# Moving 96 partition-swap DMAs of the attention stage from the GpSimd queue to the ScalarE queue

## The chip, the cores and the metric

The kernel runs on one core of a Trainium2 chip. The metric is the device time of one launch in microseconds. The engines are TensorE (PE), VectorE (DVE), ScalarE (ACT), GpSimd (POOL) and SyncE (SP). Each has its own program, and they meet only at semaphores.

## The reference, cut to what matters

The whole program is two transformer blocks over 512 tokens of width 1024: a convolution layer, a dilated-attention layer, gates and feed-forward layers. The change touches one step of the dilated attention, the partial rotation of the queries and keys:

```
q, k, v, gate = split(h @ w_in)                 # three groups of 8 heads of 64
q = partial_rope(rms_norm(q, q_norm), cos, sin) # k alike
def partial_rope(x, cos, sin):                  # only the first 16 of 64 rows turn
    x1, x2 = x[..., :8], x[..., 8:16]
    rot = concat([x1 * c - x2 * s, x2 * c + x1 * s])
    return concat([rot, x[..., 16:]])
```

The kernel keeps features on partitions and tokens along the free axis, so one 128x512 array holds two heads of 64 rows. To add `x2 * s` to `x1 * c`, rows 8 to 15 of each head have to come to the partitions of rows 0 to 7, and the other way round. DVE and ACT work within a partition, so a DMA makes that swapped copy.

## The kernel before, in words

Weights stream from HBM in 299 tiles of 512 KB through a ring of four buffers. For each tile SP issues the load, ACT writes the rounded half `w_hi` (its `prep`), DVE writes the rest `w_lo` (its `prep`), and PE multiplies three products per 128-column part. ACT and DVE work three tiles ahead of PE.

The attention stage (`begin(k, 4)` in each engine's program, about 340 to 700 us) is written as steps `c` from 0 to 4 with ten slots `j` each. In steps 0 to 3, PE projects one tile per slot: slots 0, 1, 3, 4, 5, 6 are query or key tiles (`QK_TILES`), slots 2, 7, 8 are values, slot 9 is the gate. From step 1 on the same slots also carry the softmax attention of the step before. I count the query and key tiles of a step as pieces 0 to 5 (they sit in slots 0, 1, 3, 4, 5, 6).

A piece passes through the engines in this order. PE finishes its tile in slot `j`. ACT copies it from PSUM to `at_raw` (L457, from the call in the scalar block) and squares it (L476). PE sums the squares by head in the next slot (L1649). DVE makes the variance, `head_var` (L995), two slots after the tile. ACT takes its logarithm and exponential (L495, L496), `guess_var`. DVE refines the result, `head_newton` (L988 to L990), and rotates: L1304 multiplies the swapped copy `at_pair`, L1305 to L1307 finish `at_raw` and raise `n_done`. L1304 first waits on `pair_loaded`, that is for the DMAs.

The swapped copy is made by four DMAs per piece, each of 8 partitions by 512 floats (16 KB), from `at_raw` to `at_pair[:, n % 2, :]`, where `n` is the piece counted through all steps (0 to 23). There are two `at_pair` buffers, so the DMAs of piece `n` wait until piece `n - 2` has been rotated (`n_done`). In the kernel before, POOL's whole program is these waits and 96 DMAs.

Two more waits of PE matter. In slot 8, PE turns the values of tile 7 into PSUM bank 1 (L1886), which also held the sums of squares. So it waits until `head_var` of piece 5, which DVE does in slot 8, has read that bank:

```
pe.wait_ge(var_done, len(QK_TILES) * c + (2, 6)[g])
```

And in each slot of steps 1 to 4, PE turns the probabilities of a softmax unit (L1836), for which DVE must have normalised them (L1296, L1297) after ACT's exponential (L717).

The order on each engine is that of the code. ACT's slot runs: `prep` for the tile three ahead, copy of turned probabilities `at_PT`, exponential, `guess_var`, copy of the tile, square. DVE's slot runs: `head_var`, scores, `prep`, reading a value or gate tile (L1292, L1287), normalising, `head_newton`, rotation.

Of the kernel before, what the change touches and what calls it, by code (L numbers as in the profile page):

```python
# [22 lines left out]
KC = D // P  # L23
# [8 lines left out]
HEAD = 64  # L32
# [34 lines left out]
READ0 = [4 + sum(READS[:n]) for n in range(15)]  # L67
LAST = 14
BARRIERS = ()
PAIR_CLEARED = 3  # L70
PI = 3.1415925
ROUND = 1.5 * 2.0 ** 23
TURN = (6.28125, 0.0019350051879882812, 3.019916e-07)
# [49 lines left out]
SLOTS = 10  # L123
QK_TILES = (0, 1, 3, 4, 5, 6)
# [26 lines left out]
def build(nc, weights, x_in, ple_in, pos_in, params_in, consts_in, masks_in, out, spill):  # L151
    ctx = ExitStack()
    with ctx:
# [89 lines left out]
        read_out = sem("read_out")  # L243
# [185 lines left out]

        @block.gpsimd  # L430
        def _(pool):
            pool.wait_ge(dve_out, PAIR_CLEARED)
            for c in range(4):
                for i, j in enumerate(QK_TILES):
                    n = len(QK_TILES) * c + i
                    raw = at_raw[:, 6 * (c % 2) + i, :]
                    pool.wait_ge(read_out, READ0[4] + SLOTS * c + j + 1)
                    if n >= 2:
                        pool.wait_ge(n_done, KC + n - 1)
                    for h in range(2):  # L440
                        for to, of in ((0, 8), (8, 0)):
                            pool.dma_start(at_pair[h * HEAD + to:h * HEAD + to + 8, n % 2, :],  # L442
                                           raw[h * HEAD + of:h * HEAD + of + 8, :]).then_inc(pair_loaded[n % 2], 16)


        @block.scalar
        def _(act):
            k = Counts()
# [245 lines left out]
            for c in range(5):  # L694
                a = c - 1
                for j in range(SLOTS):
                    if c < 4:
                        prep()
                        if c == 0 and j == 0:
                            logs()  # L700
                            guess(4, 1.0 / D)
                    for step in ((1, 2) if c == 4 else (2, 1)):
                        if a < 0 or not 0 <= j - step < UNITS:
                            continue
                        if step == 2:
                            act.wait_ge(t_done, UNITS * a + j - 1)
                            u = j - 2
                            if u >= 2:
                                act.wait_ge(o_done, UNITS * a + u - u % 2)
                            turned = flat(ps[:, 4:6, :])  # L710
                            bands = turned[:, 0:NQ * (P + HALF_BAND)].rearrange("p (b q) -> p b q", q=P + HALF_BAND)
                            copy(at_PT[:, u % 2, 0:NQ * HEAD].rearrange("p (b q) -> p b q", q=HEAD), bands[:, :, 0:HEAD])
                            copy(at_PT[:, u % 2, NQ * HEAD:PT_COLUMNS], turned[:, S:S + 2 * P]).then_inc(pt_done, 1)
                        else:
                            act.wait_ge(m_done, UNITS * a + j)
                            st, probs = at_st[:, (j - 1) % 4, :], unit_home(a, j - 1)
                            act.activation(probs, probs, ACT.Exp, bias=st[:, 1:2], accum_out=st[:, 2:3])\  # L717
                                .then_inc(e_done, 1)
                    v = V_SLOT.get(j - 1) if c < 4 else None
                    if j == 0 and a >= 0:  # L720
                        v = GROUPS - 1
                    if v is not None:
                        pair = c if j else a
                        act.wait_ge(v_turned, GROUPS * pair + v + 1)
                        copy(at_V[:, 3 * (pair % 2) + v, :], ps[:, 1, :]).then_inc(v_copied, 1)
                    if c < 4 and j - 1 in SUM_SLOT:
                        k.up(sq_used)
                        guess_var()
                    if j == 0 and a >= 1:
                        split(at_Yh[:, a - 1, :], 0)  # L730
                    if c < 4:
                        k.up(tile_done)
                        k.up(read_out)
                        if j == 9:
                            act.wait_ge(read_out, k.at(read_out))
                            act.activation(at_SG[:, c % 2, :], at_SG[:, c % 2, :], ACT.Silu).then_inc(gated, 1)
                            k.up(gated)
                            logs()
                        elif j in V_TILES:
                            pass  # L740
                        else:
                            act.wait_ge(tile_done, k.at(tile_done))
                            raw = at_raw[:, 6 * (c % 2) + QK_TILES.index(j), :]
                            copy(raw, ps[:, slot_bank(j), :]).then_inc(read_out, 1)
                            act.wait_ge(read_out, k.at(read_out))
                            square(raw)
            split(at_Yh[:, 3, :], 0)
            attention_over(k, unit=(m_done, e_done, t_done, pt_done, o_done), chunk=(n_done,))
            stage_end(act, "act", k, 4)
# [1555 lines left out]
```

## Time and profile before

| what | value |
|---|---|
| time, median of 3 runs | 1965.79 us (1964.72 to 1966.64) |
| the profiled execution's own time | 1964.72 us |
| its span | 1962.9 us |
| granted TensorE clock, mean | 0.989 of full speed |
| DMA queue of POOL (q0, software) | 3072 packets, 1.58 MB, 0.4% of the 16 engines |
| DMA queue of ACT (q10, hardware) | 3552 packets, 12.44 MB, 1.7% |
| DMA queue of SP (q1, hardware) | 44640 packets, 160.19 MB, 25.6% |

An engine's share of busy time says how full it is, not whether it sets the end. That is read from the chain of waits, which is followed back from the last instruction. In this profile, issuing a DMA is not counted as busy time of ACT or SP; such instructions stand in the timeline under ACTq and SPq, with the time that the issuing program is held. "to landing" is the time from issue until the data is there.

### The profile page before, as it was taken

The page shows a single profiled execution, that of the slowest core. Times are in us where ns is not written, and L with a number is a line of the kernel's source. Part 1 is how long each engine was busy: PE and PEld are TensorE (multiplying, and loading weights), DVE is VectorE, ACT ScalarE, POOL GpSimd, SP SyncE. Part 2 cuts the span into 40 slices and gives each one's busy share as a digit, 9 for nine tenths or more (in the row PEclk, how much of TensorE's full clock was granted, in tenths as well). Part 3 has the DMA queues.
Part 4 walks back from the last instruction along what each step waited for, and adds up shares of the span by engine and source line. Part 5 has one row for each costly group of instructions (what it writes and reads, how often), then busy time and mean ns, then how long its engine had stood idle before and what let it go on. Part 6 is the DMA issues. An engine that isn't in the chain of part 4 may idle for free.

```text
span 1962.9 us, 23354 instructions
## 1 busy us (share of the span) xinstructions
PE 1893.1 (96%) x8436; PEld 1474.4 (75%) x8436; DVE 1250.8 (64%) x1960; ACT 856.7 (44%) x1207; POOL 49.5 (3%) x100
## 2 busy tenths in 40 slices
PE   6999899999999899999999999999999999999999
PEld 4888587777777677888888866666766788888887
DVE  5999888867677768544443374697766654444322
ACT  5443555445445446444332244454354444343311
POOL 0000000211111000000000000000000000000000
PEclk9999999999999899999999999999999999999999
DMA  4332243322222122333333322112221332323332
GB/s 176 97 97 97 64 145 104 100 78 60 70 69 60 34 94 89 107 96 96 96 102 123 123 70 75 54 43 62 78 65 41 111 97 97 101 93 103 99 102 102
DMA packets 51346, 175.32 MB, mean 89 GB/s; under 512 B 7616, under 2 KB 7872, under 8 KB 50624
## 3 DMA queue, kind: packets, MB, share of 16 engines
q1 hardware_dynamic: 44640, 160.19, 25.6%
q10 hardware_dynamic: 3552, 12.44, 1.7%
q0 software_dynamic: 3072, 1.58, 0.4%
q8 instruction: 53, 0.87, 0.2%
q14 instruction: 29, 0.24, 0.0%
HBM read 166.32 MB, written 6.29 MB: 88 GB/s over the span
## 4 chain that ended last, share of the span: by engine, by line
PE 80%; DVE 13%; ACT 4%; issue 2%; DMA 0%; ACTq 0%; DVEq 0%
PE ps L1598 68%; PE ps L1614 2%; PE ps L1649 2%; DVE w_lo L973 2%; PE ps L1793 1%; PE ps L1836 1%; PE ps L1805 1%; DVE cv_acc L1152 1%; ACT w_hi L457 1%; PE ps L1822 1%; DVE ds_acc L1355 1%; PE ps L1991 1%; DVE X L1025 1%; DVE ds_mx L1354 1%; PE ps L2042 1%
## 5 line engine op out<-in xcount | busy, mean ns | idle before, releaser
L973 DVE TENSOR_TENSOR w_lo<-w_raw,w_hi 128x1024 fp32r<-128x1024 f32 x299 | 365.8, 1225 | 338.1 <-ACT w_hi L457 332.0
L1598 PE MATMUL ps<-H_hi,w_hi 128*128 128x512 f32 x1272 | 508.5, 400 | 1.2 <-DVE H_lo L1019 1.2
L1598 PE MATMUL ps<-H_hi,w_lo 128*128 128x512 f32 x1272 | 495.6, 390 | 0.0
L1598 PE MATMUL ps<-H_lo,w_hi 128*128 128x512 f32 x1272 | 495.1, 389 | 0.0
L457 ACT ACTIVATE w_hi<-w_raw 128x1024 fp32r<-128x1024 f32 x299 | 313.4, 1049 | 172.7 <-PE ps L1598 171.8
L1598 PEld LDWEIGHTS ps<-H_hi,w_hi 128*128 128x128 f32 x1272 | 238.9, 188 | 59.8 <-issue 9.3
L1598 PEld LDWEIGHTS ps<-H_lo,w_hi 128*128 128x128 f32 x1272 | 238.9, 188 | 55.2 <-issue 6.7
L1598 PEld LDWEIGHTS ps<-H_hi,w_lo 128*128 128x128 f32 x1272 | 238.8, 188 | 50.5
L1598 PE MATMUL ps<-mid_hi,w_lo 128*128 128x512 f32 x352 | 138.7, 394 | 0.0
L1598 PE MATMUL ps<-mid_hi,w_hi 128*128 128x512 f32 x352 | 138.7, 394 | 0.0
L1598 PE MATMUL ps<-mid_lo,w_hi 128*128 128x512 f32 x352 | 138.7, 394 | 0.0
L1598 PE MATMUL ps<-N_hi,w_hi 128*128 128x512 f32 x280 | 118.6, 424 | 0.7 <-ACT ds_P L835 0.7
L1152 DVE SCALAR_TENSOR_TENSOR cv_acc<-cv_a,par,cv_acc 128x509 f32<-128x509 f32 (+21 forms) x176 | 115.9, 728 | 1.6 <-ACT cv_acc L608 1.6
L457 ACT ACTIVATE mid_hi<-tmp 128x512 f32 x44 | 27.8, 632 | 193.3 <-DVE tmp L1110 193.3
L1598 PE MATMUL ps<-N_lo,w_hi 128*128 128x512 f32 x280 | 111.6, 399 | 0.0
L1598 PE MATMUL ps<-N_hi,w_lo 128*128 128x512 f32 x280 | 111.4, 398 | 0.0
L1598 PEld LDWEIGHTS ps<-mid_hi,w_lo 128*128 128x128 f32 x352 | 65.8, 187 | 16.4
L1598 PEld LDWEIGHTS ps<-mid_hi,w_hi 128*128 128x128 f32 x352 | 65.8, 187 | 16.2
L1598 PEld LDWEIGHTS ps<-mid_lo,w_hi 128*128 128x128 f32 x352 | 65.8, 187 | 16.2
L1106 DVE TENSOR_TENSOR tmp<-ps,rx 128x512 f32<-128x512 f32 x44 | 30.4, 691 | 66.2 <-PE ps L1598 66.2
L1598 PEld LDWEIGHTS ps<-N_hi,w_hi 128*128 128x128 f32 x280 | 53.6, 191 | 22.9 <-issue 9.3
L442 POOL DMA_DIRECT2D at_pair<-at_raw x96 | 49.3, 520 | 591.2 <-ACT at_raw L457 529.3
(342 smaller groups left out, 2717.0 us busy)
## 6 DMA issues: line engine op xcount, KB each, us to landing
w_raw<-weights SPq DMA_DIRECT2D x299, 512.0 KB, 3.5
X<-x ACTq DMA_DIRECT2D x4, 512.0 KB, 12.0
pl_P<-spill ACTq DMA_DIRECT2D x1, 2048.0 KB, 7.9
spill<-X ACTq DMA_DIRECT2D x8, 256.0 KB, 2.0
X<-spill ACTq DMA_DIRECT2D x2, 1024.0 KB, 5.2
out<-X SPq DMA_DIRECT2D x8, 256.0 KB, 4.5
at_pair<-at_raw POOLq DMA_DIRECT2D x96, 16.0 KB, 1.8
pl_raw<-ple SPq DMA_DIRECT2D x2, 512.0 KB, 13.0
```

What stands on the lines that cost most here:

```text
L442: pool.dma_start(at_pair[h * HEAD + to:h * HEAD + to + 8, n % 2, :], raw[h * HEAD + of:h * HEAD + of + 8, :]).then_inc(pair_loaded[n % 2], 16)
L457: return act.activation(out_ap, in_ap, ACT.Copy)
L973: dve.tensor_tensor(w_lo[:, s, :], w_raw[:, s, :], w_hi[:, s, :].bitcast(F32), ALU.subtract)\
L1025: dve.scalar_tensor_tensor(X[:, m:m + n, :], src, scale, X[:, m:m + n, :], ALU.mult, ALU.add)\
L1106: dve.tensor_tensor(tmp[:, j, :], ps[:, bank_of(k.n["prep"] - AHEAD - 1), :], rx[:, :], ALU.mult).then_inc(read_out, 1)
L1152: instr = dve.scalar_tensor_tensor(acc, a[:, 0:S - t], w, acc, ALU.mult, ALU.add)
L1354: link(dve.max(ds_mx[:, :], acc))
L1355: link(dve.match_replace(acc, ds_mx[:, :], acc, TAKEN))
L1598: mm = pe.matmul(ps[:, bank, :], w, x, start=first and n == 0 and q == 0, stop=last and n == len(blocks) - 1 and q == 2)
L1614: mm = pe.matmul(ps[:, banks[which], :], w, x[:, b, :], start=b == 0 and q == 0, stop=b == KC - 1 and q == 2, skip_group_check=True)
L1649: pe.matmul(ps[:, bank, :], ones if lhsT is None else lhsT, sq[:, (k.n[sq_done] - 1) % 2, :], start=c == 0, stop=c == n - 1).then_inc(sq_u ...
L1793: mm = pe.matmul(ps[:, near_bank(a, near), :], at_raw[rows, q, r:S:4], at_raw[rows, q + 1, :], start=True, stop=True)
```

## The change

POOL's DMAs and waits are taken out, and ACT issues the same 96 DMAs with the same sources, destinations and semaphores. They stand behind the square of the piece. The wait for the rotation of piece `n - 2` comes with them. `normed` is the value of `n_done` at the start of the stage.

```diff
         @block.gpsimd
         def _(pool):
-            pool.wait_ge(dve_out, PAIR_CLEARED)
-            for c in range(4):
-                for i, j in enumerate(QK_TILES):
-                    n = len(QK_TILES) * c + i
-                    raw = at_raw[:, 6 * (c % 2) + i, :]
-                    pool.wait_ge(read_out, READ0[4] + SLOTS * c + j + 1)
-                    if n >= 2:
-                        pool.wait_ge(n_done, KC + n - 1)
-                    for h in range(2):
-                        for to, of in ((0, 8), (8, 0)):
-                            pool.dma_start(at_pair[h * HEAD + to:h * HEAD + to + 8, n % 2, :],
-                                           raw[h * HEAD + of:h * HEAD + of + 8, :]).then_inc(pair_loaded[n % 2], 16)
+            k = Counts()
...
                             act.wait_ge(read_out, k.at(read_out))
+                            n = len(QK_TILES) * c + QK_TILES.index(j)
                             square(raw)
+                            if n == 0:
+                                act.wait_ge(dve_out, k.at(dve_out))
+                            if n >= 2:
+                                act.wait_ge(n_done, normed + n - 1)
+                            for h in range(2):
+                                for to, of in ((0, 8), (8, 0)):
+                                    act.dma_start(at_pair[h * HEAD + to:h * HEAD + to + 8, n % 2, :],
+                                                  raw[h * HEAD + of:h * HEAD + of + 8, :])                                        .then_inc(pair_loaded[n % 2], 16)
```

On ACT, in step 0, slots 5 and 6 (pieces 4 and 5), this stood before; the bracket names the semaphores that a row waits on:

```order
L457 ACTIVATE at_raw<-ps 128x512 [waits tile_done]
L476 ACTIVATE sq<-at_raw 128x512 [waits sq_used,read_out]
L457 ACTIVATE w_hi<-w_raw 128x1024 [waits tile_done,landed1]
L495 ACTIVATE r0<-var 128x512 [waits var_done]
L496 ACTIVATE r0<-r0 128x512 [waits act_chain]
L457 ACTIVATE at_raw<-ps 128x512 [waits tile_done]
L476 ACTIVATE sq<-at_raw 128x512 [waits sq_used,read_out]
L457 ACTIVATE w_hi<-w_raw 128x1024 [waits tile_done,landed2]
L495 ACTIVATE r0<-var 128x512 [waits var_done]
```

The same place in the changed kernel, whose line numbers are 8 lower there:

```order
L449 ACTIVATE at_raw<-ps 128x512 [waits tile_done]
L468 ACTIVATE sq<-at_raw 128x512 [waits sq_used,read_out]
L746 DMA at_pair<-at_raw 8x512 [waits n_done]
L746 DMA at_pair<-at_raw 8x512 x3
L449 ACTIVATE w_hi<-w_raw 128x1024 [waits tile_done,landed1]
L487 ACTIVATE r0<-var 128x512 [waits var_done]
L488 ACTIVATE r0<-r0 128x512 [waits act_chain]
L449 ACTIVATE at_raw<-ps 128x512 [waits tile_done]
L468 ACTIVATE sq<-at_raw 128x512 [waits sq_used,read_out]
L746 DMA at_pair<-at_raw 8x512 [waits n_done]
L746 DMA at_pair<-at_raw 8x512 x3
L449 ACTIVATE w_hi<-w_raw 128x1024 [waits tile_done,landed2]
```

Four DMAs, the first with a wait on `n_done`, now stand between each square and the next `w_hi` with the next logarithm. On POOL, the start of the attention stage before, after which the program of the changed kernel has nothing left:

```order
L442 DMA at_pair<-at_raw 8x512 [waits read_out,dve_out]
L442 DMA at_pair<-at_raw 8x512 x3
L442 DMA at_pair<-at_raw 8x512 [waits read_out]
L442 DMA at_pair<-at_raw 8x512 x3
L442 DMA at_pair<-at_raw 8x512 [waits n_done,read_out]
L442 DMA at_pair<-at_raw 8x512 x3
```

Nothing moves on DVE, PE or SP.

## Rows read from the trace of the kernel before

**Rows 1.** The page, busy time, share of the span and instructions of each engine.

```profile
PE   1893.1 (96%) x8436; PEld 1474.4 (75%) x8436; DVE 1250.8 (64%) x1960; ACT 856.7 (44%) x1207; POOL 49.5 (3%) x100
```

**Rows 2.** Stretches: length, PE, PEld, DVE, ACT, POOL busy, clock, DMA, GB/s.

```profile
340.00:404.00 64.00, 63.49 (x267) 48.76 (x266) 54.99 (x79) 32.84 (x45) 12.41 (x24) 1.00 0.36 107
```

**Rows 3.** Instructions on at_pair: durations ns min/median/max, first and last start; idle.

```profile
L442 POOL DMA_DIRECT2D at_pair<-at_raw x96: 518/518/636, 345.5 to 640.4; - x96
L1304 DVE TENSOR_TENSOR at_pair<-at_pair,at_S x12: 691/693/694, 357.3 to 646.8; 128x512 f32<-128x512 f32 x12
...
  DVE at_raw L1307: 61.9, 8
...
DMA to landing us min/median/max: 1.7/1.8/4.3
```

**Rows 4.** DMA issues of SP and ACT; two lines by line, three from the timeline.

```profile
L418 SPq DMA_DIRECT2D w_raw<-weights x292: 332/333/343, 8.0 to 1921.7; - x146
...
L551 ACTq DMA_DIRECT2D spill<-X x8: 326/327/343, 1025.6 to 1133.4; - x8
...
339.26 0.63 ACTq L690 DMA_DIRECT2D at_near<-masks  x1
...
339.92 0.63 ACTq L691 DMA_DIRECT2D at_far<-masks  x1
340.65 1.06 ACT L457 ACTIVATE w_hi<-w_raw 128x1024 fp32r<-128x1024 f32 x1 [0.24 <-issue]
```

**Rows 5.** Timeline of ACT, step 0: start us, us, engine, line.

```profile
367.64 0.63 ACT L476 ACTIVATE sq<-at_raw 128x512 f32<-128x512 f32 x1
368.17 1.04 ACT L457 ACTIVATE w_hi<-w_raw 128x1024 fp32r<-128x1024 f32 x1
369.12 0.61 ACT L495 ACTIVATE r<-var 128x512 f32<-128x512 f32 x1
...
376.14 0.63 ACT L495 ACTIVATE r<-var 128x512 f32<-128x512 f32 x1 [0.59 <-DVE var L995]
```

**Rows 6.** Timeline of DVE, step 0, slots 4 to 8.

```profile
369.32 1.23 DVE L973 TENSOR_TENSOR w_lo<-w_raw,w_hi 128x1024 fp32r<-128x1024 f32 x1 [0.41 <-ACT w_hi L457]
370.46 0.69 DVE L988 TENSOR_TENSOR rs<-r 128x512 f32<-128x512 f32 x1
...
374.69 0.69 DVE L1307 TENSOR_TENSOR at_raw<-at_raw,rs 128x512 f32<-128x512 f32 x1
...
377.48 0.69 DVE L988 TENSOR_TENSOR rs<-r 128x512 f32<-128x512 f32 x1
...
381.71 0.69 DVE L1307 TENSOR_TENSOR at_raw<-at_raw,rs 128x512 f32<-128x512 f32 x1
...
386.03 0.69 DVE L1292 TENSOR_TENSOR at_SG<-ps,rx 128x512 f32<-128x512 f32 x1 [1.64 <-PE ps L1598]
...
391.58 0.69 DVE L995 SCALAR_TENSOR_TENSOR var<-ps,ex 128x512 f32<-128x512 f32 x1
```

**Rows 7.** The chain that ended last, at slot 8 of step 0.

```profile
392.42 0.72 PE ps L1886 x4
```

**Rows 8.** Timeline of ACT, step 2, slots 5 and 6.

```profile
539.28 0.64 ACT L457 ACTIVATE at_PT<-ps 128x256 f32<-128x256 f32 x2
542.93 0.94 ACT L717 ACTIVATE at_Sm<-at_Sm,at_st 128x768 f32<-128x768 f32 x1 [3.01 <-DVE at_st L1270]
```

**Rows 9.** Timeline of DVE, step 2, slots 5 to 7.

```profile
539.87 0.69 DVE L1307 TENSOR_TENSOR at_raw<-at_raw,rs 128x512 f32<-128x512 f32 x1
...
545.29 0.68 DVE L988 TENSOR_TENSOR rs<-r 128x512 f32<-128x512 f32 x1
...
549.51 0.69 DVE L1307 TENSOR_TENSOR at_raw<-at_raw,rs 128x512 f32<-128x512 f32 x1
...
555.79 0.15 DVE L1296 RECIPROCAL at_st<-at_st 128x1 f32<-128x1 f32 x1
```

**Rows 10.** Timeline of PE, step 2, slot 7.

```profile
556.66 0.33 PE L1836 MATMUL ps<-con,at_Sm 128*128 128x128 f32 x1 [0.48 <-DVE at_Sm L1297]
```

More of the change, by code:

```diff
@@ L69 @@
 BARRIERS = ()
-PAIR_CLEARED = 3
 PI = 3.1415925
@@ L431, in _ @@
         def _(pool):
-            pool.wait_ge(dve_out, PAIR_CLEARED)
-            for c in range(4):
-                for i, j in enumerate(QK_TILES):
-                    n = len(QK_TILES) * c + i
-                    raw = at_raw[:, 6 * (c % 2) + i, :]
-                    pool.wait_ge(read_out, READ0[4] + SLOTS * c + j + 1)
-                    if n >= 2:
-                        pool.wait_ge(n_done, KC + n - 1)
-                    for h in range(2):
-                        for to, of in ((0, 8), (8, 0)):
-                            pool.dma_start(at_pair[h * HEAD + to:h * HEAD + to + 8, n % 2, :],
-                                           raw[h * HEAD + of:h * HEAD + of + 8, :]).then_inc(pair_loaded[n % 2], 16)
+            k = Counts()
+            for stage in BARRIERS:
+                stage_end(pool, "pool", k, stage)
         @block.scalar
```

## The prediction

> **What bounds the kernel now.** I read the busy shares first: PE is busy 96% of the span, ACT 44%, POOL 3% [rows 1]. So a microsecond counts only if PE ends up waiting for it. Next, the stretches: in step 0 of the attention stage, PE is busy 63.49 of 64.00 us, DVE 54.99 and ACT 32.84 [rows 2]. DVE has little room there, and ACT looks half empty. Last, the instructions on `at_pair`. POOL issues 96 DMAs of 518 ns, the data lands 1.8 us later (at most 4.3), and the first is issued at 345.5, while the first rotation starts at 357.3 [rows 3]. No idle time of DVE is put down to a landing, so the transfers are well hidden. Eight times in 24, POOL waited for the rotation L1307 on DVE, 61.9 us in all [rows 3]. Those are pieces 4 and 5 of each step, and that wait cost nothing, since nothing stood behind it on POOL. After the change it stands on ACT.
>
> **What goes.** POOL's 96 issues (49.5 us with its other work [rows 1]) are on nobody's path. Removing them gives back nothing inside the span. What a launch spends outside the span is 1964.7 - 1962.9 = 1.8 us. If POOL's queue had a share in that, it could return at most that. I take 0.
>
> **What comes: the time ACT is held per piece.** The trace has no small hardware DMA from SBUF to SBUF, so I bound its issue. Isolated issues take 0.33 us for 256 KB on ACT and for 512 KB on SP alike [rows 4], so size hardly counts. The two mask loads took 0.63 each, starting 0.66 apart [rows 4]. The next `w_hi` began 0.10 after the second had ended, with 0.24 idle put down to "issue": issues do hold the arithmetic behind them. From below, I have no row of a DMA with few rows, and the bound is zero. I take 0.33, the value of 300 issues, with the 0.03 gap between the two mask loads (339.92 - 339.26 - 0.63). Call the burst of four Q. It is 4 x 0.33 + 3 x 0.03 = 1.41 us, between 0 and 4 x 0.63 + 0.09 = 2.61.
>
> The Trainium skill, Perfetto Trace Analysis, section "DMA Instruction — HWDGE (DVE, Sync)", says the issuing sequencer is free for the next instruction only when the descriptors are generated and excess semaphore increments pushed. The trace agrees, by the 0.10 behind the second mask load. If instead ACT could run on during the burst, the sum below would be 0.
>
> **Step 0, slot by slot.** Behind the burst stand `w_hi`, on which DVE's `w_lo` waits, and the logarithm L495, on which DVE's refinement L988 waits. After the wait, both are late, and DVE's next rotation is late, on which ACT's next burst waits.
>
> - Slot 4 (piece 3). No real wait. The square starts at 367.64 and the first DMA about 0.09 later, as at the masks (339.26 against an instruction at 339.17; I estimate the same). `w_hi` then starts at 367.73 + 1.41 + 0.10 = 369.24 in place of 368.17 [rows 5], 1.07 late. DVE was already waiting for it [rows 6], so DVE is 1.07 late, that is Q - 0.34.
> - Slot 5 (piece 4). The rotation of piece 2 ended at 374.69 + 0.69 = 375.38 [rows 6], now 376.45. With 0.05 for the semaphore, the burst runs to 377.91 and `w_hi` starts at 378.01. L495 follows 0.95 later (369.12 - 368.17 [rows 5]), at 378.96. DVE's L988 follows L495 by 377.48 - 376.14 = 1.34 [rows 5, 6], at 380.30 in place of 377.48: 2.82 late, or 2Q.
> - Slot 6 (piece 5). The rotation of piece 3 ended at 381.71 + 0.69 = 382.40, now 385.22. The burst runs from 385.27 to 386.68, `w_hi` starts at 386.78. `w_lo` starts 1.15 later (369.32 - 368.17) and holds DVE 1.14 (370.46 - 369.32 [rows 6]), to 389.07. Then comes L1292 of tile 7, which stood at 386.03 because it waited 1.64 for PE. It is 3.04 late, or 3Q - 1.19. DVE runs without idle time from there to L995 of piece 5.
> - Slot 8. L995 moves from 391.58 to 394.62. PE's L1886 waits for exactly this one; it began at 392.42, 0.15 after L995 had ended [rows 6, 7]. So it begins at 395.46.
>
> PE loses 3.04 us here. Everything after it moves with PE, so DVE and ACT have their old lead again.
>
> **Steps 1 to 3.** Here slots are longer. I take step 2. The rotation ends at 539.87 + 0.69 = 540.56 [rows 9]; burst to 542.02; `w_hi` at 542.12; the `at_PT` copies 0.95 later; the exponential 0.60 after that, at 543.67 in place of 542.93; L495 0.94 later and L988 1.34 after that, at 545.95 in place of 545.29 [rows 8, 9]. That is 0.66, or Q - 0.75. The next rotation ended at 549.51 + 0.69 = 550.20, now 550.86; burst from 550.91 to 552.32; `w_hi` 552.42; exponential at 553.97; its sum is ready about 1.10 later, at 555.07. DVE wants it at 555.79 for L1296 [rows 9], so 0.72 is left over, and PE, which waits 0.48 for that product at 556.66 [rows 10], sees nothing. In general PE loses 2Q - 3.54 per step, from Q = 1.77 on.
>
> The bursts of slots 0, 1, 3 and 4 wait for no rotation. Each makes `w_hi` late once, by about 1.07 as in slot 4 above. The softmax work of PE makes these slots longer than those of step 0, and the cover is that PE uses a tile's weights only three slots after `prep`. I cost them at nothing; without that cover it would be 1.07 each.
>
> **Sum.** 3.0 + 3 x 0 = 3.0 us. On the profiled execution's own 1964.7 this is 1967.7. That execution lies 1.1 under the median of 1965.8, on which the sum gives 1968.8. I say 1968.0.
>
> **The rivals.**
>
> - The small issue is nearly free. A DMA of 8 rows has a sixteenth of the rows of those that took 0.33. If the issue time is mostly per row, Q falls below 0.40, 3Q - 1.19 is under zero, and the time stays at 1965 to 1966. For it: no row shows a small issue. Against it: 256 KB and 512 KB took the same 0.33, which looks like a fixed price. In the Trainium skill, DMA: Bandwidth & Descriptors, section "Why a DMA increments its semaphore by 16 and not by 1", an 8-row transfer would use 8 of the 16 engines and the sequencer would write the other increments. No row here shows which way that moves the price.
> - The burst is dear, and the kernel is slower. At the 0.63 of the masks, Q is 2.61. Step 0 costs 3 x 2.61 - 1.19 = 6.6 us. Steps 1 to 3 now lose too, 2 x 2.61 - 3.54 = 1.7 each at L1836 in slot 7. The sum is 11.7, the time 1976 to 1977. It is over 0.2% (3.9 us) from Q = 1.71 on, that is from 0.40 per issue. For it: the only two ACT issues just ahead of this stage took 0.63. Against it: they move 1.1 MB in rows of another layout.
> - Freeing POOL gains. The transfers would land earlier or POOL's start-up would vanish. Against it: nothing waits for the landing, and at most 1.8 us lie outside the span: 1963 to 1964. The Trainium skill, SBUF — State Buffer, section "SBUF: two separate sides", warns that DVE's fast modes starve descriptor writing on POOL. The trace does not agree: POOL's issues took 518 ns in the median and 636 at most, beside a DVE that was busy 55 of 64 us. By that rule something would be won only if DVE waited for a landing, which it does not.
>
> **How the numbers follow.** Q near 1.41 (1.1 to 1.7): 50%. Issue nearly free, or up to a microsecond of loss: 25%. Dear burst: 20%. A gain: 5%. This kernel's runs can tell about 0.2% from no change, that is 3.9 us. Slower holds the dear burst and the upper edge of the first case, 25%; faster about 4%; the same 71%. For the range, the low end of 1964 takes in the free issue at the profiled execution's own level. The high end of 1974 stands for Q = 2.35 (5.86 + 3 x 1.16 = 9.3 by the sum, on 1964.7). That leaves out some 8% above and as much below.
>
> **What would show it.** Right: ACTq rows of about 0.33 us at `at_pair`; the burst of piece 4 in step 0 ending near 378; L1292 at about 389; a PE wait of 3 us ahead of L1886 at 392, put down to DVE's L995; no new PE wait in steps 1 to 3; POOL empty. Wrong: issue rows under 0.1, with L1886 still at 392.4; issue rows over 0.45, with L1836 waiting 1 us or more in slot 7 of each step; or a first DMA issued long after the rotation it waits for.

## The result, and the profile after

| | before | after |
|---|---|---|
| device time, median of four runs (us) | 1966.22 | 1983.39 |
| lowest and highest run (us) | 1964.72, 1966.81 | 1981.53, 1984.99 |
| the profiled execution, its span (us) | 1964.72, 1962.9 | 1984.48, 1982.7 |
| mean granted clock of TensorE | 0.989 | 0.983 |

The kernel got slower, by 17.2 us. The ratio is 1.009, with a 95% interval of 1.0075 to 1.0106. I had forecast 1968 and given a range up to 1974, so the result lies outside it. The direction and the place were those of my "dear burst" rival, and the size went beyond it as well.

First the busy shares, then the instructions on `at_pair`. The columns are those of [rows 1] and [rows 3]. In the kernel after, DVE and PE lines are numbered one higher than before, and ACT's lines eight lower (`w_hi` is L449, the logarithm L487).

```profile
PE 1902.5 (96%) x8436; PEld 1480.5 (75%) x8436; DVE 1251.7 (63%) x1960; ACT 856.0 (43%) x1207; POOL 0.2 (0%) x4
```

```profile
L746 ACTq DMA_DIRECT2D at_pair<-at_raw x96: 631/632/1242, 344.6 to 659.8; - x96
```

PE, DVE and ACT are busy for about as long as before. ACT's shares say nothing, because the 61 us in which it issued DMAs are not counted as busy. The second row is the heart of the case. An issue takes 632 ns in the median and never less than 631, where I had taken 330. Four in a row take 2.62 us (four times 0.632, with 0.03 between them), where I had taken 1.41.

The stretches of [rows 2] and of step 2, after the change (length, then PE, PEld, DVE, ACT and POOL busy, granted clock, DMA share, GB/s), the ten microseconds around the new waits, and one microsecond behind two of them:

```profile
340.00:404.00 64.00, 56.92 (x228) 43.44 (x228) 50.21 (x72) 29.20 (x41) 0.00 (x0) 0.95 0.31 99
480.00:560.00 80.00, 76.98 (x392) 59.62 (x392) 54.81 (x108) 36.20 (x63) 0.00 (x0) 0.96 0.20 63
390.00:400.00 10.00, 5.95 (x27) 4.74 (x27) 8.23 (x11) 4.19 (x6) 0.00 (x0) 0.90 0.16 56
400.00:410.00 10.00, 10.00 (x33) 7.54 (x33) 7.68 (x12) 4.30 (x6) 0.00 (x0) 0.76 0.33 104
480.00:490.00 10.00, 10.00 (x33) 7.33 (x32) 7.16 (x13) 3.59 (x7) 0.00 (x0) 0.67 0.23 73
...
401.00:402.00 1.00, 1.00 (x4) 0.80 (x3) 0.97 (x2) 0.98 (x3) 0.00 (x0) 0.50 0.61 156
482.00:483.00 1.00, 1.00 (x4) 0.77 (x4) 0.98 (x2) 0.03 (x1) 0.00 (x0) 0.50 0.03 8
```

In step 0, PE is busy 56.9 of 64 us where it was busy 63.5 [rows 2]. That part of the loss is idle time. The fourth row shows a second part: PE is busy all the time, at a clock of 0.76, and gets 33 matmuls done, where the kernel before gets 43 done in the same ten microseconds. The last two rows show what that mean is made of: the clock granted there is 0.50.

ACT in step 0, slots 4 to 6 (start, us, engine, line; what answers to [rows 5]):

```profile
367.70 0.63 ACT L468 ACTIVATE sq<-at_raw 128x512 f32<-128x512 f32 x1
367.70 2.62 ACTq L746 DMA_DIRECT2D at_pair<-at_raw  x4
370.43 1.06 ACT L449 ACTIVATE w_hi<-w_raw 128x1024 fp32r<-128x1024 f32 x1 [2.09 <-issue]
...
377.68 2.62 ACTq L746 DMA_DIRECT2D at_pair<-at_raw  x4
380.40 1.06 ACT L449 ACTIVATE w_hi<-w_raw 128x1024 fp32r<-128x1024 f32 x1 [5.53 <-PE ps L1599]
381.37 0.62 ACT L487 ACTIVATE r<-var 128x512 f32<-128x512 f32 x1
...
387.65 2.62 ACTq L746 DMA_DIRECT2D at_pair<-at_raw  x4
390.37 1.06 ACT L449 ACTIVATE w_hi<-w_raw 128x1024 fp32r<-128x1024 f32 x1 [6.57 <-issue]
```

DVE in the same slots (what answers to [rows 6]), with the instruction that PE waits for last:

```profile
376.95 0.69 DVE L1308 TENSOR_TENSOR at_raw<-at_raw,rs 128x512 f32<-128x512 f32 x1
...
381.56 1.22 DVE L974 TENSOR_TENSOR w_lo<-w_raw,w_hi 128x1024 fp32r<-128x1024 f32 x1 [3.19 <-ACT w_hi L449]
...
386.93 0.69 DVE L1308 TENSOR_TENSOR at_raw<-at_raw,rs 128x512 f32<-128x512 f32 x1
...
391.53 1.23 DVE L974 TENSOR_TENSOR w_lo<-w_raw,w_hi 128x1024 fp32r<-128x1024 f32 x1 [3.19 <-ACT w_hi L449]
392.68 0.68 DVE L1293 TENSOR_TENSOR at_SG<-ps,rx 128x512 f32<-128x512 f32 x1
...
398.22 0.69 DVE L996 SCALAR_TENSOR_TENSOR var<-ps,ex 128x512 f32<-128x512 f32 x1
```

This is the ring that I had drawn. DVE ends a rotation at 377.64. The burst that waited for it starts at 377.68 and ends at 380.30. `w_hi` follows 0.10 later, and DVE's `w_lo`, which needs it, starts at 381.56 after 3.19 us without work. DVE's next rotation ends at 387.62. The ring turned every 7.0 us before ([rows 6]: 374.69, 381.71) and turns every 10.0 now (376.95, 386.93).

PE at the two places where that arrives, in slots 7 and 8 of step 0 (what answers to [rows 7]), and the products after them:

```profile
388.40 1.12 PE L1650 MATMUL ps<-sq,con 128*128 128x512 f32 x2 [2.15 <-DVE var L996]
...
399.06 1.10 PE L1887 MATMUL ps<-con,at_SG 128*128 128x128 f32 x4 [4.05 <-DVE var L996]
...
400.81 0.63 PE L1599 MATMUL ps<-H_hi,w_lo 128*128 128x512 f32 x1
401.24 0.63 PE L1599 MATMUL ps<-H_hi,w_hi 128*128 128x512 f32 x1
```

PE waits 2.15 and 4.05 us, 6.2 in all. A smaller new wait of 0.57 us stands ahead of them, in slot 3 (L1887 at 360.9, for the variance of piece 1); it comes from the early bursts. The last two rows then start 0.43 apart and last 0.63. The same products last 0.39 and start 0.23 apart elsewhere in this trace. That is the lower of the clock's two levels, 1.2 in place of 2.4 GHz, and it agrees with the 0.50 in the stretch above.

PE in slot 7 of step 2 (what answers to [rows 10]):

```profile
570.53 1.09 PE L1823 MATMUL ps<-at_PT,at_V 128*64 128x128 f32 x24 [1.01 <-ACT at_PT L449]
572.58 0.87 PE L1837 MATMUL ps<-con,at_Sm 128*128 128x128 f32 x6 [0.95 <-DVE at_Sm L1298]
```

These two stand in each of the steps 1 to 3 (477.8 and 479.8, 570.5 and 572.6, 662.2 and 664.3). Together they are 1.96 us, where the one wait before was 0.48.

Last, PE's waits in the whole stage (340 to 730), summed by what was waited for: us in total, times, the longest. After:

```profile
PE ps L1837 <- DVE at_Sm L1298: 13.9, 14, 1.5
PE ps L1887 <- DVE var L996: 4.6, 2, 4.1
PE ps L1823 <- ACT at_PT L449: 4.3, 6, 1.0
...
PE ps L1650 <- DVE var L996: 2.1, 1, 2.1
```

Before:

```profile
PE ps L1836 <- DVE at_Sm L1297: 11.6, 10, 1.5
...
PE ps L1822 <- ACT at_PT L457: 0.9, 2, 0.5
```

Before, the list has no wait for `var`. The four rows sum to 24.9 us, the two of before to 12.5: the waits grew by 12.4 (a further group, L1794 for `at_st`, shrank from 3.1 to 2.7). For the length of the stage I take the time from the last write to `spill` ahead of it (252.5 before) to the read-back of `spill` right behind it (699.1 before); this holds some 88 us ahead of step 0 too. It is 465.9 us in place of 446.6, so 19.3 longer. What the clock adds can be read in stretches of ten microseconds: (1 - granted clock) x 10, summed from 340 to 730. It is 15.2 after (eight stretches) and 6.9 before (three, all from 660 on), 8.3 more. The two parts sum to 20.7, against 19.3 measured; they overlap a little, since the clock is also low in stretches where PE waits. So waits are some three fifths of the loss, and the lower clock most of the rest.

Read by stretches of one microsecond, the 8.3 is a difference of two things. The changed kernel has four stretches at 0.50 that the kernel before has not: 6.8 us from 397.9, 6.8 from 479.8, 3.4 from 616.4 and 6.8 from 664.2. Behind the softmax tail of the stage it has 6.8 us at 0.50 (from 688), where the kernel before has 13.6 (from 668). Three of the new stretches stand at the new waits. The one at 616.4 does not, and the kernel with issues but no wait, below, has a like one at 602.6; so that part isn't tied to the new waits.

### The profile page after: what moved, and what is told of

It reads as the page before. It is cut to its first block, busy times and chain, and to the rows that moved or that the text cites. A ratio compares the mean times of both kernels' runs of the same rounds, so it can differ in the third digit from the quotient of the medians.

```text
span 1982.7 us, 23331 instructions
## 1 busy us (share of the span) xinstructions
PE 1902.5 (96%) x8436; PEld 1480.5 (75%) x8436; DVE 1251.7 (63%) x1960; ACT 856.0 (43%) x1207; POOL 0.2 (0%) x4
## 4 chain that ended last, share of the span: by engine, by line
PE 73%; DVE 16%; ACT 5%; issue 3%; ACTq 2%; DMA 0%; DVEq 0%
PE ps L1599 63%; PE ps L1615 2%; DVE w_lo L974 2%; ACTq L746 2%; PE ps L1650 1%; ACT w_hi L449 1%; PE ps L1794 1%; PE ps L1837 1%; DVE cv_acc L1153 1%; DVE ds_acc L1356 1%; PE ps L1992 1%; DVE rs L991 1%; DVE rs L990 1%; DVE X L1026 1%; DVE rs L989 1%
## 5 line engine op out<-in xcount | busy, mean ns | idle before, releaser
L449 ACT ACTIVATE w_hi<-w_raw 128x1024 fp32r<-128x1024 f32 x299 | 313.7, 1050 | 250.4 <-PE ps L1599 176.6
L1599 PEld LDWEIGHTS ps<-H_hi,w_hi 128*128 128x128 f32 x1272 | 240.3, 189 | 60.9 <-issue 10.1
L449 ACT ACTIVATE mid_hi<-tmp 128x512 f32 x44 | 27.8, 632 | 193.4 <-DVE tmp L1111 193.4
L1599 PEld LDWEIGHTS ps<-N_lo,w_hi 128*128 128x128 f32 x280 | 53.8, 192 | 13.7 <-issue 2.2
```

Source lines behind the costliest of these rows:

```text
L449: return act.activation(out_ap, in_ap, ACT.Copy)
L1599: mm = pe.matmul(ps[:, bank, :], w, x, start=first and n == 0 and q == 0, stop=last and n == len(blocks) - 1 and q == 2)
```

## The experiments

My theory after the result: an issue between two places in SBUF holds ACT for 0.63 us, and the bursts of pieces 4 and 5, which wait for a rotation, turn that into a ring between ACT and DVE that ends in PE's waits and, behind them, in a lower clock. The rivals: it is the wait for the rotation by itself; it is the time that ACT is held, wherever it is; it is the transfer on a hardware queue. All ratios are to the kernel before on the same chip, with a 95% interval.

### The wait alone

POOL issues again; ACT only waits where it would issue.

```
+            pool.wait_ge(dve_out, PAIR_CLEARED)
+            for c in range(4):
...
+                            pool.dma_start(at_pair[...], raw[...]).then_inc(pair_loaded[n % 2], 16)
...
                             if n >= 2:
                                 act.wait_ge(n_done, normed + n - 1)
-                            for h in range(2):
-                                for to, of in ((0, 8), (8, 0)):
-                                    act.dma_start(at_pair[...], raw[...])
```

> POOL issues the 96 DMAs as before, and ACT only waits for the rotation of piece n - 2 behind each square, without issuing anything. Chain theory (the loss is ACT held 2.6 us per burst, 4 issues of 0.63 us, and it counts only where a burst begins at the end of a rotation): the wait alone costs nothing, since ACT's next w_hi then starts about 1 us late in slots 5 and 6 and DVE has that much room: 1965 to 1967 us, ratio 1.000. Rival (the wait itself, which ties ACT to DVE, is the loss): most of the 17 us, 1978 or more.

Measured: 1965.35 against 1965.66, ratio 0.9997 [0.9987, 1.0006]; the stage takes 446.5 us, as before. The wait costs nothing by itself. The 61.9 us that POOL waited [rows 3] said nothing about a price on ACT.

### Two issues per piece, and three

Leaves out the transfers of the second head's swap, so half the rotation's input.

```
-                            for h in range(2):
+                            for h in range(1):
```

> As the changed kernel, but only two of the four DMAs per piece, those of the first head; the second head's rows get no swapped copy, so part of the rotation is left out. A burst is 1.29 us. Chain theory: step 0 loses 3 x 1.29 - 1.19 = 2.7 us, steps 1 to 3 nothing, and PE's stall is too short for much loss of clock: 1968 to 1970 us. Rival (loss in proportion to the number of issues): 8.7 us, 1975. Rival (the landing of the DMAs or the wait is the loss, not the issues): 1980 or more.

Measured: 1971.33 against 1965.66, 1.0029 [1.0019, 1.0039]. This is PE in slot 8 of step 0, and ACT's issues in that kernel:

```profile
PE ps L1887 <- DVE var L996: 2.7, 1, 2.7
```

```profile
L746 ACTq DMA_DIRECT2D at_pair<-at_raw x48: 631/632/1233, 344.9 to 643.7; - x48
```

Two issues are 1.29 us. My own formula for step 0, 3Q - 1.19, gives 2.68 for that, and the wait is 2.69. Steps 1 to 3 show no new wait; 2Q - 3.54 is negative there. The stage is 4.0 longer: the wait, and 3.4 us with a granted clock of 0.50 around the products behind it (395.1 to 398.5), which cost half of that. The timed runs say 5.7, above the 1968 to 1970 that I expected. From the read-back behind the stage to the next read-back of `spill`, the profiles take either about 828 us (before: 828.0) or about 830.6 (this kernel: 830.7), whatever is done in the stage: the kernel with the wait alone has 830.5 and loses nothing in its timed runs. So I read the steps from the stage.

Three issues leave out one of the four transfers.

```
-                                for to, of in ((0, 8), (8, 0)):
+                                for to, of in ((0, 8), (8, 0))[:2 - h]:
```

> As the changed kernel with three DMAs per piece; one of the second head's two swapped parts is left out, so part of the rotation is not done. A burst is 1.96 us. Chain theory: step 0 waits 3 x 1.96 - 1.19 = 4.7 us, steps 1 to 3 each 2 x 1.96 - 3.54 = 0.4, together 5.8, and 2 to 3 us of lower clock behind the step 0 stall: 1973 to 1975 us. Rival (in proportion to the issues): 13 us, 1979. Rival (straight line between two and four per piece, 5.7 and 17.6): 11.7 us, 1977.

Measured: 1974.88 against 1964.74, 1.005 [1.0036, 1.0063]. In step 0 the waits are 1.02 and 3.40, so 4.4, where the formula gives 4.7. In steps 1 to 3, L1837 waits 0.95 (0.48 before). The stage is 7.7 longer. With 0, 2, 3 and 4 issues per piece the loss is 0, 5.7, 10.1 and 17.2 us. It grows faster than the number of issues.

### The burst one slot later

The same 96 issues, but behind the next `w_hi` and the next logarithm on ACT.

```
                         guess_var()
+                    if c < 4 and j in SUM_SLOT:
+                        n, raw = pending
+                        if n >= 2:
+                            act.wait_ge(n_done, normed + n - 1)
...
+                                act.dma_start(at_pair[...], raw[...])
```

> As the changed kernel, same 96 issues on ACT with the same waits, but each burst stands one slot later, behind w_hi and the logarithm and exponential of the next slot. Chain theory: neither w_hi nor guess_var stands behind the wait and the burst any more, and the rotation of piece n - 2 is long done: 1965 to 1968 us. Rival (63 us of issue time on ACT cost in themselves, or hardware DMAs from SBUF to SBUF slow the weight loads): 1978 or more.

Measured: 1965.04 against 1965.66, 0.9997 [0.9988, 1.0006]. ACT in the place of the rows above:

```profile
368.20 1.04 ACT L449 ACTIVATE w_hi<-w_raw 128x1024 fp32r<-128x1024 f32 x1
369.15 0.62 ACT L487 ACTIVATE r<-var 128x512 f32<-128x512 f32 x1
369.80 0.63 ACT L488 ACTIVATE r<-r 128x512 f32<-128x512 f32 x1
369.81 2.62 ACTq L727 DMA_DIRECT2D at_pair<-at_raw  x4
373.38 0.60 ACT L449 ACTIVATE at_raw<-ps 128x512 f32<-128x512 f32 x1 [2.94 <-PE ps L1602]
```

The burst is just as long, 2.62 us, and costs nothing. It ends at 372.43, in a gap in which ACT waits for PE until 373.38 anyway, and `w_hi` starts at 368.20 as in [rows 5]. This is the strongest single result. It excludes the time held as such, the transfers and ACT's hardware queue. What costs is that `w_hi` and the logarithm stand behind the burst and its wait.

In the later place the wait for the rotation is over when ACT gets there: the burst of the next slot starts at 376.84, and the rotation that it needs ended at about 375.4, as in [rows 6]. So this kernel takes away both the wait and what stood behind it, and the two are told apart only by the other runs.

### SyncE issues

The same transfers on SP's queue, between its weight loads.

```
+            for t in range(RING * first, RING * last):
...
+                    sp.wait_ge(read_out, READ0[4] + SLOTS * c + j + 1)
+                    if n >= 2:
+                        sp.wait_ge(n_done, KC + n - 1)
...
+                            sp.dma_start(at_pair[...], raw[...]).then_inc(pair_loaded[n % 2], 16)
```

> The 96 DMAs are issued by SP between its weight loads, behind the load that follows w_lo of the same slot; ACT and POOL issue none. Chain theory: nothing urgent is queued behind them on SP, and a weight load is needed only some slots later: 1965 to 1967 us. The price per issue shows whether 0.63 us belongs to ACT (then SP shows about 0.33) or to the transfer (then 0.63 here too). Rival (the hardware queue's transfers land late or disturb the weight stream): 1975 or more.

Measured: 1964.59 against 1965.66, 0.9995 [0.9986, 1.0004]. SP's issues:

```profile
L434 SPq DMA_DIRECT2D at_pair<-at_raw x96: 624/625/792, 345.9 to 639.9; - x96
```

The price per issue is the same on SP, so it doesn't belong to ACT. On SP nobody stands behind it who is in a hurry.

### Which pieces

ACT issues pieces 0 to 3 of each step and POOL pieces 4 and 5; then the other way round.

```
+                            if n % len(QK_TILES) in (0, 1, 2, 3):
                                 if n >= 2:
                                     act.wait_ge(n_done, normed + n - 1)
```

> ACT issues the bursts of pieces 0 to 3 of each step (64 DMAs, whose wait for the rotation is over when ACT gets there), POOL those of pieces 4 and 5. Chain theory: each such burst makes w_hi late once by 1.6 to 2.3 us and the slot takes it up: 1965 to 1968 us. Rival (loss in proportion to the issues on ACT): two thirds of 17 us, 1977.

```
+                            if n % len(QK_TILES) in (4, 5):
                                 if n >= 2:
                                     act.wait_ge(n_done, normed + n - 1)
```

> The other half of the split: ACT issues only the bursts of pieces 4 and 5 of each step (32 DMAs, which wait for a rotation), POOL the other 64. Chain theory: nearly the whole loss stays: some 10 to 16 us, 1976 to 1982 us, with PE waiting ahead of L1886 in step 0 and for normalised probabilities in slot 7 of each later step. Rival (in proportion to the issues): a third of 17 us, 1972.

Measured: the early pieces, 64 issues, 1968.23 against 1965.49, 1.0014 [1.0005, 1.0023], with 0.9 us of new waits in step 0 and a stage 0.7 longer. Of the eleven timed runs, four took 1966.1 to 1966.3, which fits those waits, at a mean granted clock of 0.988 to 0.989; one took 1967.7, and six took 1968.2 to 1971.2, at 0.986 to 0.987. The profiled one is of the six, and 2.7 us of its excess lie behind the stage (830.7 against 828.0), where these issues don't stand. So only about 0.8 of the 2.7 us is traced to the bursts. The late pieces, 32 issues, 1983.33 against 1965.49, 1.009 [1.0076, 1.0103], just above the 1982 that I had as the upper end. A third of the issues makes the whole loss. PE's waits with the late pieces (from 340 to 730):

```profile
PE ps L1849 <- DVE at_Sm L1310: 13.0, 10, 1.5
PE ps L1899 <- DVE var L1008: 4.1, 1, 4.1
PE ps L1835 <- ACT at_PT L460: 4.0, 5, 1.0
...
PE ps L1662 <- DVE var L1008: 0.8, 1, 0.8
```

The waits are those of the kernel after, but for 1.3 us in slot 7 of step 0 (0.8 for 2.15). The granted clock is 0.50 for 3.4 us from 399.7 and for 6.8 us each from 478.2 and 570.4, so at the waits of steps 0, 1 and 2.

### What an issue costs

The kernel before, with six bursts of four DMAs more on ACT in the last stage, where ACT has room: 8 or 128 rows of 2 KB, between two places in SBUF, from SBUF to HBM, and from HBM to SBUF.

```
+                        if kind == "ss":
+                            act.dma_start(H_hi[128 - rows:128, ...], con[0:rows, 0:S])
+                        elif kind == "sd":
+                            act.dma_start(scrap[0:rows, ...], con[0:rows, 0:S])
+                        else:
+                            act.dma_start(H_lo[0:rows, ...], scrap[0:rows, ...])
```

> The kernel before, with 24 more DMAs issued by ACT in the last stage, in bursts of four with nothing else in flight on its queue: 8 rows SBUF to SBUF, 128 rows SBUF to SBUF, 128 rows SBUF to HBM, 128 rows HBM to SBUF, 8 rows SBUF to HBM, 8 rows HBM to SBUF, each row 2 KB. Fixed-price theory: 0.33 us for all, and 0.63 in the attention stage would be due to something else there. Kind theory: 0.63 for SBUF to SBUF whatever the rows, 0.33 where HBM is one end. Burst theory: the first of each four 0.33, the others more. The total time is of no interest here.

```profile
1865.96 3.28 ACTq L961 DMA_DIRECT2D H_hi<-con  x4
1881.36 2.50 ACTq L961 DMA_DIRECT2D H_hi<-con  x4
1896.77 1.84 ACTq L963 DMA_DIRECT2D scrap<-con  x4
1912.16 1.78 ACTq L965 DMA_DIRECT2D H_lo<-scrap  x4
1927.56 1.33 ACTq L963 DMA_DIRECT2D scrap<-con  x4
1942.96 1.99 ACTq L965 DMA_DIRECT2D H_lo<-scrap  x4
```

The first two bursts stay in SBUF, the first with 8 rows, the second with 128. Sixteen times the rows are not dearer: 2.50 against 3.28, of which 0.6 is the first issue's extra (1.27 us, as the first of the stage takes 1.24). The median of the eight is 0.632. To HBM (third and fifth row) it is 0.330, from HBM (fourth and sixth) 0.454, between 0.27 and 0.68. To HBM the burst of 128 rows took 1.84 and that of 8 rows 1.33, or about 0.44 and 0.31 per issue, so rows count a little there. Inside SBUF they don't set the price, and my "nearly free" rival was wrong at its root. What the bursts differ in is where their ends lie, in SBUF or in HBM. The Trainium skill, DMA: Bandwidth & Descriptors, section "Why a DMA increments its semaphore by 16 and not by 1", has a transfer of 8 rows on 8 of the 16 engines, with the sequencer writing the other increments. The trace doesn't show that this makes the issue dearer: without the first issue's extra, 8 rows took 2.65 and 128 rows 2.50 inside SBUF, and to HBM 8 rows were the cheaper. The probe is one profile, and for reads from HBM it leaves open why some take 0.3 and the masks 0.63 [rows 4].

### Which steps, and the clock

The immediate burst in step 0 alone, the later place in steps 1 to 3; and the reverse.

```
+                    if c < 4 and j in SUM_SLOT and not (c == 0):
+                        n, raw = pending
...
+                            if (c == 0):
                                 if n >= 2:
                                     act.wait_ge(n_done, normed + n - 1)
```

> As the changed kernel in step 0 (burst right behind the square); in steps 1 to 3 the burst stands one slot later, behind w_hi and the logarithm and exponential, where it was seen to cost nothing. Chain theory: step 0 loses 3 x 2.62 - 1.19 = 6.6 us of PE waiting, ahead of L1650 and L1887, and some 2.5 us more because PE's clock stands at its lower level for a few us afterwards: 9 us, 1974 to 1976. Rival (the clock has no part in it): 6.6, 1972. Rival (the loss is spread evenly over the steps): a quarter of 17.5, 1970.

> The reverse of first_step_only: in step 0 the burst stands one slot later, in steps 1 to 3 right behind the square as in the changed kernel. Chain theory: each of the three steps loses about 1.5 us ahead of L1837 and L1823 in slots 6 and 7, 4.5 to 5 in all, and the rest of the 17.5 us that first_step_only does not show comes from PE's lower clock behind these stalls: 1972 to 1976 us. Rival (no clock): 1970.

Measured: step 0 alone 1973.04 against 1964.74, 1.0051 [1.0038, 1.0065], the stage 9.3 longer. Steps 1 to 3 alone, 1974.44 against 1964.79, 1.0048 [1.0035, 1.0062], the stage 8.9 longer, with waits of 1.0 and 0.95 in slot 7 of each. The first is just under the 1974 to 1976 that I expected, the second inside its range. By the medians their losses are 8.3 and 9.6 and sum to 17.9; by the ratios they are 10.0 and 9.4, each give or take 2.7. So within the noise the two are the whole, and steps 1 to 3, which I had at zero, are about half of it.

Then step 0 alone once more, with products of constants (results unused) that keep PE busy where it would wait: five ahead of L1887 and two ahead of the product of piece 5.

```
+            def fill_in(times):
+                for _ in range(times):
+                    pe.matmul(ps[:, 3, :], ones, con[:, 0:S], start=True, stop=True)
...
+                            if c == 0 and g == 1:
+                                fill_in(5)
...
+                        if n == 5:
+                            fill_in(2)
```

> As first_step_only, and PE does needless products of constants into a free bank while it would stand still: 2 ahead of the sum of squares in slot 7 and 5 ahead of the turning of the values in slot 8, 0.86 us each. Clock theory: PE is never idle for long, the granted clock stays at 2.4 GHz from 395 to 410 us, and the kernel is 2 to 3 us faster than first_step_only though PE does more: 1972 to 1973. Rival (the clock fell for another reason): the clock falls as before, and the time is that of first_step_only or up to 0.5 us more.

Step 0 alone, without the filling, then with it (columns as in the stretches above):

```profile
390.00:400.00 10.00, 5.93 (x25) 4.74 (x24) 9.02 (x13) 4.55 (x7) 0.00 (x0) 0.83 0.18 54
400.00:410.00 10.00, 10.00 (x36) 7.65 (x35) 7.27 (x11) 4.62 (x6) 0.00 (x0) 0.83 0.36 106
```

```profile
390.00:400.00 10.00, 10.00 (x39) 6.66 (x38) 8.21 (x11) 4.17 (x6) 0.00 (x0) 1.00 0.19 56
400.00:410.00 10.00, 10.00 (x43) 7.75 (x43) 7.87 (x13) 5.44 (x7) 0.00 (x0) 1.00 0.32 102
```

The filled kernel does no slow product there and its stage is 2.2 us shorter (453.7 against 455.9). So the profile shows that the low clock at this place follows from PE's idle time. The timed runs don't tell the two apart: 1973.28 against 1964.74, 1.0041 [1.0027, 1.0055], an interval that overlaps that of step 0 alone; the gain of 2 to 3 us that I expected isn't seen in them. Part of the reason may be the time behind the stage, which is 3.0 us longer in the profile of the filled kernel (830.7 against 827.7). That the clock costs 2 us in step 0 is therefore shown in one profile each and not by times.

### The issues without their wait

POOL makes the real transfers; ACT issues four others per piece, of 8 rows of 192 bytes into unused memory, and doesn't wait for the rotation.

```
-                            if n >= 2:
-                                act.wait_ge(n_done, normed + n - 1)
...
+                            if n:
+                                act.wait_ge(scratched, 64 * n)
+                            for q in range(4):
+                                act.dma_start(scratch[8:16, q, :], con[0:8, 48 * q:48 * q + 48])
```

> POOL issues the 96 real DMAs as before. ACT issues four further ones per piece behind the square, SBUF to SBUF, 8 rows of 192 bytes, which wait only for those of the piece before. Chain theory: ACT is held as long as in the changed kernel (2.6 us per piece, and 0.63 per issue in spite of the shorter rows), but not tied to the end of a rotation, so w_hi is late once per piece and no delay feeds the next: 1965 to 1968 us. Rival (held time alone is the loss): 1980 or more.

Measured: 1970.53 against 1964.74, 1.0031 [1.0019, 1.0044], above the 0 to 3 us that I expected.

```profile
L752 ACTq DMA_DIRECT2D scratch<-con x96: 631/632/1241, 344.5 to 641.0; - x96
```

```profile
PE ps L1893 <- DVE var L1002: 2.2, 2, 1.9
```

192 bytes per row cost the same 0.632 as 2 KB. Held time without the wait for the rotation costs at most 5.8 us, and with it 17. In this profile the stage is 3.7 longer: 2.2 us of waits, and 3.4 us at a clock of 0.50 (from 602.6), which cost half of that. The wait of 1.86 at 362 isn't all due to held time. The test brought a wait of its own, for the landing of the burst before: it holds the burst of piece 1 back to 350.78, while the changed kernel, whose waits are over by then, starts it at 349.49 and has only 0.57 us of waiting at the same place. So about 1.3 us of the loss belong to the test. The rest of the 5.8 lies behind the stage (830.7 against 828.0), as with the early pieces. So I had called the early bursts covered a little too readily, although pieces 0 to 3 alone cost only 2.7. A version in which the real transfers need no wait for the rotation (four `at_pair` buffers) wasn't tried.

## Why the prediction was wrong

**The step that failed** is "What comes: the time ACT is held per piece", where I wrote "I take 0.33". It measured 0.632, and Q 2.62 in place of 1.41. The bound that I gave from above, 2.61, was nearly met. I had two groups of rows [rows 4] and took the larger, 300 issues that all have one end in HBM, although none of them stays in SBUF. The two masks were on the same engine, just ahead of the stage, and twice as dear. Nothing in the trace told what set the difference, and against that the choice of 0.33 was a vote by count. The argument against the dear burst, that the masks "move 1.1 MB in rows of another layout", rested on rows and size. The probe shows that rows don't count inside SBUF, and 16 KB are as dear as 256. I gave the dear burst 20%.

**What goes, and the freed POOL:** right. POOL's issues gave nothing back: with POOL empty and the bursts one slot later, the ratio is 0.9997. In the rival of the freed POOL I wrote "The trace does not agree"; the 518 ns of POOL's issues beside DVE's work are too little for that, since no row says whether this work ran in the modes that are meant. That ACT is held during the burst: right, and the 0.10 us from its end to `w_hi` came out as in [rows 4]. This is the rule of the Trainium skill's Perfetto Trace Analysis, section "DMA Instruction — HWDGE (DVE, Sync)", that I had weighed: the sequencer is free only after its descriptors are generated. The trace agrees a second time, by `w_hi` 0.10 behind each burst of 2.62.

**Step 0:** the ring, its waits and its place were right. With Q = 2.62 my working has DVE's rotations of pieces 2 and 3 late by Q - 0.34 = 2.28 and 2Q = 5.24, and L1292 and L995 by 3Q - 1.19 = 6.67. Measured are 2.26, 5.22, 6.65 and 6.64 (376.95, 386.93, 392.68 and 398.22, against [rows 6]). With two and three issues per piece, L1887 begins 2.63 and 4.67 late, where the formula gives 2.68 and 4.69. So the working fits to a few hundredths once Q is right. PE, 0.2 us late already by the wait in slot 3, lost it in two parts, 6.2 together, as L1650 waited 2.15 for piece 4's variance in slot 7 before L1887 waited in slot 8. I had looked at one place only, but the delay arrives once.

**Steps 1 to 3:** "2Q - 3.54 per step, from Q = 1.77 on" is a term that I set to zero because of Q. With 2.62 it gives 1.7 per step. Measured are 0.95 - 0.48 at the turning of `at_Sm` (L1837), and 1.01 at L1823, which I hadn't named: 1.5 per step. The runs by steps show that this half of the loss is real. The 0.95 all but meets the mark "L1836 waiting 1 us or more in slot 7", which I had given for the case of over 0.45 per issue.

**Early bursts:** costed at nothing. The early pieces alone cost 2.7 us, of which 0.9 is seen as waits, most of it in slot 3 of step 0 (0.57 in the changed kernel). It is a small error, and in a formula for Q = 2.62 it should have been checked again.

**The term that was missing:** the clock. At its own Q my dear burst gave 11.7 us, and PE's waits grew by 12.4, but the time grew by 17.2. In this stage of the kernel before, PE's clock is below 0.99 only from 660 on, behind the softmax tail. At each wait of 2.7 us or more ahead of L1887 in slot 8 it was 0.50 for 3.4 us (two and three issues per piece, the late pieces) or for 6.8 us (the changed kernel, step 0 alone). At two of the three pairs of 1 us in slot 7 it was so for 6.8 us in the changed kernel and with the late pieces, and for 3.4 and 6.8 us with steps 1 to 3 alone. PE stands still in a part of some of these stretches; in the rest its products go at half the rate. No such stretch came at the 2.15 us in slot 7 of step 0, nor at the 1.86 us in the kernel with issues but no wait. What decides whether one comes, and whether it is 3.4 or 6.8 us long, these runs don't show. I gave the stage's new waits their length and not what PE does after them. With the right price, my working would still have come out 5.5 us too low.

## What to carry to other kernels

Price a DMA issue on an engine by a row of the same kind, both ends in the same memories; where there is none, take both groups of rows seriously and put the chances between them, since size and rows may not be what tells them apart. Then ask what stands behind the issue on that engine: the same 2.62 us cost 17 us ahead of the conversion that others wait for, and nothing one slot later, where the engine was idle anyway. A wait that was harmless on an idle engine becomes a link of a ring when it moves to one whose output the waited-for engine needs, and new idle time of a busy TensorE should be costed with the slower products that may follow it (here 1.7 or 3.4 us for each stretch at the lower level).

## What was not expected of the hardware

- The issue of a DMA with both ends in SBUF held ACT for 0.632 us in the median, with 8 or 128 rows and 192 bytes or 2 KB per row, and SP for 0.625 (8 rows of 2 KB). To HBM the median was 0.33 on ACT (bursts of four: 1.33 us with 8 rows, 1.84 with 128). POOL's issues of the same transfers took 0.518.
- The first such issue on ACT took 1.23 to 1.27 us. On SP none took more than 0.79.
- Around a PE wait of 4.1 us, the clock was at the 1.2 GHz level for 6.8 us with the change in step 0 alone (396.5 to 403.3; PE was busy for the last 5.0 of them) and for 3.4 us with the late pieces. Around one of 2.7 us it was 3.4 us. With the wait filled by unused products it never fell there.
- Two waits of 1.0 and 0.95 us, one product group apart, could do as much: 6.8 us at that level, from 479.8 in the changed kernel. In step 2 of the same kernel the same pair did nothing.
